# A fused fp32 model on one Trainium2 core: jobs in other places, and the S5 scan's result in PSUM

## The reference

```python
# layer 0: mixer = conv (31 taps, layernorm, silu) and retention heads, then @ w_out
# layer 1: mixer = S5, both directions, 64 groups of 16 channels, 64 complex states
for direction in (0, 1):
    bu_re = jnp.einsum('sgc,gpc->sgp', us, bb_re[direction])
    bu_im = jnp.einsum('sgc,gpc->sgp', us, bb_im[direction])
    _, _, h_re, h_im = lax.associative_scan(
        _s5_combine, (a_re, a_im, bu_re, bu_im), reverse=(direction == 1), axis=0)
    y = y + (jnp.einsum('sgp,gcp->sgc', h_re, cr[direction])
             - jnp.einsum('sgp,gcp->sgc', h_im, ci[direction]))
z = jax.nn.gelu(y + d_skip * u)
return (z @ w_glu_a) * jax.nn.sigmoid(z @ w_glu_b)
```

## Time and profile before

| | before |
|---|---|
| median of 3 executions | 1332.55 us (1329.34 to 1334.72) |
| the profiled execution, own time | 1337.0 us |
| its span | 1335.2 us, 24456 instructions |
| mean granted clock of TensorE | 0.956 |
| busy: PE, PEld | 1233.7 us (92%), 1143.0 us (86%) |
| busy: DVE, ACT, POOL | 856.9 (64%), 530.6 (40%), 410.0 (31%) |
| moved by DMA | 258.20 MB, mean 193 GB/s |

### The profile page before, as it was taken

The page is one execution under the profiler, slowest core; times in us unless marked ns, Lnnn a source line. Parts: engine busy times, 40 slices in busy tenths (PEclk is TensorE's granted clock), DMA queues, the critical chain, the costliest instruction groups (busy, mean ns, idle before and its releaser), DMA issues.

```text
span 1335.2 us, 24456 instructions
## 1 busy us (share of the span) xinstructions
PE 1233.7 (92%) x10696; PEld 1143.0 (86%) x10696; DVE 856.9 (64%) x946; ACT 530.6 (40%) x663; POOL 410.0 (31%) x573
## 2 busy tenths in 40 slices
PE   4898897999998878898999999998998999999998
PEld 4785685999998848787899999698787999999998
DVE  6699963886567558845597543556856467556553
ACT  2130232444233244343455432448267644544241
POOL 7999638398788218700000000000000012000000
PEclk7899898999998889999999999999798999999999
DMA  9962667588977645256265554345141445455551
GB/s 349 389 256 94 236 219 262 187 306 304 338 286 273 225 138 172 75 171 229 68 249 190 189 179 175 122 156 190 43 147 64 151 166 189 161 174 177 182 192 64
DMA packets 120251, 258.20 MB, mean 193 GB/s; under 512 B 5056, under 2 KB 19024, under 8 KB 120016
## 3 DMA queue, kind: packets, MB, share of 16 engines
q1 hardware_dynamic: 91184, 196.18, 41.8%
q10 hardware_dynamic: 25504, 46.81, 9.6%
q0 software_dynamic: 3456, 13.63, 2.7%
HBM read 241.93 MB, written 14.68 MB: 192 GB/s over the span
## 4 chain that ended last, share of the span: by engine, by line
PE 68%; DVE 11%; POOL 8%; DMA 5%; issue 3%; ACT 3%; SPq 1%; DVEq 0%; POOLq 0%; ACTq 0%
PE bank L1864 68%; DVE big L1403 4%; POOL tabw L714 2%; POOL tabw L711 2%; POOL big L781 2%; DMA ring<-in_w_in 1%; DMA ada_slot<-in_ada_w 1%; DVE ada_acc L1293 1%; POOL prep L719 1%; DMA ring<-in_w_fc 1%; DVE rstd L1303 1%; POOL big L774 1%; SPq L585 1%; DVE ring_split L1346 1%; ACT ada_slot_split L874 1%
## 5 line engine op out<-in xcount | busy, mean ns | idle before, releaser
L1864 PE MATMUL bank<-squares_split,ring_split 128*128 128x256 f32 x1056 | 300.7, 285 | 0.0
L1864 PEld LDWEIGHTS bank<-squares_split,ring_split 128*128 128x128 f32 x1056 | 204.5, 194 | 0.0
L787 POOL TENSOR_TENSOR y_cat<-y_cat,tmp 128x512 f32<-128x512 f32 x8 | 11.1, 1388 | 536.9 <-DVE tmp L1782 536.9
L1293 DVE SCALAR_TENSOR_TENSOR ada_acc<-ada_slot,cact,ada_acc 128x512 f32<-128x512 f32 x152 | 126.9, 835 | 5.1
L1864 PE MATMUL bank<-ada_slot_split,ring_split 128*128 128x256 f32 x432 | 122.2, 283 | 0.0
L1346 DVE TENSOR_TENSOR ring_split<-ring,ada_slot_split 128x2048 fp32r<-128x2048 f32 (+1 forms) x32 | 72.1, 2257 | 56.9 <-ACT ada_slot_split L874 56.9
L1864 PE MATMUL bank<-big_split,ring_split 128*128 128x256 f32 x352 | 100.1, 284 | 0.0
L1303 DVE RECIPROCAL rstd<-bank 128x512 f32<-128x512 f32 (+1 forms) x21 | 56.0, 2668 | 51.1 <-ACT bank L805 51.0
L1864 PE MATMUL bank<-big_split,ada_slot_split 128*128 128x256 f32 x296 | 85.5, 289 | 0.0
L1864 PEld LDWEIGHTS bank<-ada_slot_split,ring_split 128*128 128x128 f32 x432 | 82.9, 192 | 0.0
L1346 DVE TENSOR_TENSOR ring_split<-ring,tabw_split 128x2048 fp32r<-128x2048 f32 x22 | 50.4, 2291 | 49.6 <-ACT tabw_split L874 49.6
(11 more groups left out here) (420 smaller groups left out, 3879.9 us busy)
## 6 DMA issues: line engine op xcount, KB each, us to landing
...
```

Source lines behind the costliest of these rows:

```text
L1293: stt(acc, w[:, i, :], cact[:, i:i + 1], acc, ALU.mult, ALU.add)\
L1864: return pe.matmul(*args, skip_group_check=True, **kw)
```

## The change

The same work, in other places, and some in another engine or buffer.

1. *S5 loop.* The scan writes into the bank that held its own drive, DVE does both rotated products from there, POOL only the sum. v, dd and z get fixed banks, outside of the rotation; z and its reader use half a bank.
2. *S5 weights.* `wt` and `kl` are separate groups with places of their own, the first pair now ahead of `wo0.0` and the second behind `ms1`; POOL's c part waits for `kl` of the block before, and loads its input later. ACT's copies are split likewise.
3. *Projections.* `project` and `project_split` loop over input tiles outside and output tiles inside; `wo0.0/wo0.1` and `f1.0.0/f1.0.1` run as pairs. `ada7` and `ada8` follow the first pair. The inverses of `ms0`, `ms1` stay in PSUM.
4. *Start.* The first four modulation loads come in two halves, the S5 scalars before `ada_acc(4)`.
5. *Memory.* Its panel is loaded before the GLU's, its squares and mean (`mms`) come before `uu`, its norm right behind the loop. `uu` goes in two halves.
6. *GLU and norm.* `squares(3)` stand before the next split, and `KEEP_BUSY` is shorter.
7. *Second block.* `fv0`, `fv1` before `go0`; roots written to SBUF (`ROOT_PLACES`); ACT copies the linear attention's result; `nr4`, `nr5` together; two rows picked before the loop; the gates' splits use another order of buffers.

The diff, cut to its core:

```diff
-KEEP_BUSY = {"f1.0.0": 4, "uu0": 6, "ga0": 4, "ms3": 6}
+KEEP_BUSY = {"f1.0.0": 2, "uu0": 4, "ms3": 2}
...
-ADA_AFTER = {3: 10, 6: 11, 8: 12, 11: 13, 13: 14, 15: 15}
+ADA_AFTER = {3: 10, 6: 11, 8: 12, 11: 13, 15: 14}
...
-S5_AFTER = {4: 2, 10: 3, 15: 4}
-SIDE_ADA = {0: 16, 1: 17, 3: 18, 4: 19, 5: 20, 6: 21}
-SIDE_S5 = {1: 5, 3: 6, 5: 7}
+WT_AFTER = {2: 2, 6: 3, 10: 4, 14: 5}
+KL_AFTER = {4: 2, 8: 3, 12: 4}
+SIDE_ADA = {0: 15, 1: 16, 2: 17, 3: 18, 4: 19, 5: 20, 6: 21}
+SIDE_WT = {1: 6, 3: 7}
+SIDE_KL = {0: 5, 2: 6, 4: 7}
 
...
-            "wo0.0", "ada7", "wo0.1", "wt0.0", "kl0", "wt0.1", "ada8", "wo0.2", "ada9", "wo0.3", "wt1.0", "kl1", "wt1.1", "ms1"]
+            "wt0.0", "wt0.1", "kl0", "wo0.0", "wo0.1", "ada7", "ada8", "wo0.2", "ada9", "wo0.3", "ms1", "wt1.0", "wt1.1", "kl1"]
...
+            jobs.append(f"kl{SIDE_KL[b]}")
+    jobs += [f"f2.0.{p}" for p in range(4)] + ["ms2", "mms"]
...
-             "nr0", "nr1", "fk1", "cs0", "cs1", "at0", "at1", "go0", "gor0", "nr2", "nr3", "go1", "gor1",
-             "fv0", "fv1", "mq0", "mq1"]
+             "nr0", "nr1", "fk1", "cs0", "cs1", "at0", "at1", "fv0", "fv1", "go0", "nr2", "nr3", "gor0", "go1", "mq0", "gor1", "mq1"]
...
+            if name in S5_JOBS:
+                n = int(name[1:]) if name[0] != "d" else int(name[2:]) + 3
+                return bank[n % 6 if name[0] == "v" or name in ("dd0", "dd1", "dd2") else 7 if name == "dd3" else 6 + n % 2]
...
         ffn_panels(0)
+        panels.append(("mem", a["mem"].rearrange("(k p) t -> p k t", p=P), KT, T, ("memn", None)))
         for i in range(2):
             cols_panel(f"ga{i}", a["w_glu_a"], 512 * i, 512, f"ga{2 * i + 1}")
             cols_panel(f"gb{i}", a["w_glu_b"], 512 * i, 512, f"gb{2 * i + 1}")
-            if i == 0:
-                panels.append(("mem", a["mem"].rearrange("(k p) t -> p k t", p=P), KT, T, ("memn", None)))
         cols_panel("mk", a["w_mem_kv"], 0, 512, "mk1")
...
-        freed = {f"ms{n}": ("rstd", n + 1) for n in range(7)}
+        freed = {f"ms{n}": ("hn", 8 * n + 8) if n < 2 else ("rstd", n + 1) for n in range(7)}
...
+        def inverse_of(job, width):
+
+            return ps(job)[:, 0:width] if job in ("ms0", "ms1") else rs[:, 0:width]
+
+        ROOT_PLACES = {"nr0": (tabw, 0), "nr1": (tabw, 512), "nr2": (tabw, 1024), "nr3": (tabw, 1536), "gor0": (go_sq, 0), "gor1": (go_sq, 512)}
...
-                sp.dma_start(ada_slot(k), ada_source(k)).then_inc(ada_in(k)[0], 16)
+                sp.dma_start(ada_slot(k)[:, 0:4], ada_source(k)[:, 0:4]).then_inc(s(f"ada_first{k}"), 16)
+                sp.dma_start(ada_slot(k)[:, 4:8], ada_source(k)[:, 4:8]).then_inc(ada_in(k)[0], 16)
...
                 if k:
+                    job_wait(pool, f"kl{k - 1}")
                     pool.wait_ge(s("wout_out"), 16 * k)
+                if k == 0:
+                    pool.wait_ge(s("sd"), 4)
+                if k < 7:
+                    pool.dma_start(bc[(k + 1) % 2], a["s5_bc"][k + 1]).then_inc(s(f"bc_in{(k + 1) % 2}"), 16)
...
-            for n in range(17):
-                if n < 16:
-                    pool.wait_ge(s("s5p"), 2 * n + 2)
-                    if n >= 2:
-                        pool.wait_ge(s("s5g"), n - 1)
-                    pb = pbuf[n % 2]
-                    pool.tensor_tensor(wbuf[n % 2], pb[:, 0], pb[:, 1], ALU.add).then_inc(s("s5w"), 1)
-                if n >= 1:
-                    m = n - 1
-                    tab = tabs[m // 2 % 3][:, 4 * (m % 2):4 * (m % 2) + 4]
-                    pool.wait_ge(s("s5g"), m + 1)
-                    if m >= 4:
-                        pool.wait_ge(s("s5y"), m - 3)
-                    pool.tensor_tensor(rotated(m)[:, 1], gbuf[m % 2][:, :, ::-1, :], tab[:, :, 2:0:-1, :], ALU.mult).then_inc(s("s5r"), 1)
+            for n in range(16):
+                pool.wait_ge(s("s5p"), 2 * n + 2)
+                if n >= 2:
+                    pool.wait_ge(s("s5g"), n - 1)
+                pb = pbuf[n % 2]
+                pool.tensor_tensor(wbuf[n % 2], pb[:, 0], pb[:, 1], ALU.add).then_inc(s("s5w"), 1)
...
+            s5_weights_out(0)
+            s5_lags_out(0)
             for i in range(4):
                 act.wait_ge(s("lny"), i + 1)
                 act.activation(yt3[:, i, :], conv[:, i, :], ACT.Silu, bias=col("cln_b", i)).then_inc(s("yconv"), 1)
             ada_load(act, 9)
-            s5_weights_out(0)
             ada_load(act, 10)
             split_high(0)
             split_high(1)
-            squares(1)
+            squares(1, False)
+            split_high(2)
+            root("ms1")
+            shift(1)
+            s5_weights_out(1)
+            s5_lags_out(1)
             ada_load(act, 11)
-            s5_weights_out(1)
-            shift(1)
...
                     split_high(FC + u)
-                    if u in (2, 6, 10):
-                        s5_weights_out(5 + u // 4)
+                    if u in (2, 5):
+                        s5_weights_out(6 + u // 4)
                 if b >= FC2 + 3:
                     act.wait_ge(s("row_panel"), rows_before[place[f"f2.0.{b - 3}"]])
                 act.wait_ge(s("fsq_act"), 2 * b + 2)
                 act.activation(fc2_high(b), big3[:, 4 * b:4 * b + 4, :], ACT.Copy).then_inc(s("b_high"), 1)
+                if b in (2, 3, 5):
+                    s5_lags_out({2: 5, 3: 6, 5: 7}[b])
                 if b < 6:
                     ada_load(act, 16 + b)
+            act.wait_ge(s(f"panel{place['mem'] % RING}"), 16 * (place["mem"] // RING + 1))
+            for c in range(4):
+                act.activation(mem_sq[:, 512 * c:512 * c + 512].rearrange("p (k t) -> p k t", k=2),
+                               mem_x[:, 2 * c:2 * c + 2, :], ACT.Square).then_inc(s("msq"), 1)
             squares(2)
...
-            for n in range(3):
+            decay_row(0)
+            shift(2)
+            root("mms")
+            for n in (1, 2):
                 decay_row(n)
-            shift(2)
...
+            squares(3, False)
             split_high(SECOND)
+            root("ms3")
             split_high(SECOND + 1)
-            squares(3)
             shift(3)
...
             norm(0, False)
+            s5_scalars()
             ada_acc(4)
-            s5_scalars()
...
-                    if m >= 2:
-                        dve.wait_ge(s("s5r"), m - 1)
                     dve.wait_ge(s("decay"), 4 * m + 4)
-                    flat = (view.rearrange("p q c t -> p (q c t)") for view in (gbuf[m % 2], wbuf[m % 2]))
-                    result, source = flat
+                    source = wbuf[m % 2].rearrange("p q c t -> p (q c t)")
+                    result = ps(f"v{m}")[:, :]
                     dve.tensor_tensor_scan(result, decays[m % 3], source, 0.0, ALU.mult, ALU.add).then_inc(s("s5g"), 1)
                     dve.wait_ge(s("s5g"), m + 1)
                     if m >= 4:
                         dve.wait_ge(s("s5y"), m - 3)
-                    tt(rotated(m)[:, 0], gbuf[m % 2], tab[:, :, 0:1, :].broadcast_to([P, 4, 2, 64]), ALU.mult).then_inc(s("s5q"), 1)
-                if n >= 5 and n % 2:
-                    z_low((n - 5) // 2)
-            z_low(6)
-
+                    scan = result.rearrange("p (q c t) -> p q c t", q=4, c=2)
+                    tt(rotated(m)[:, 0], scan, tab[:, :, 0:1, :].broadcast_to([P, 4, 2, 64]), ALU.mult).then_inc(s("s5q"), 1)
+                    tt(rotated(m)[:, 1], scan[:, :, ::-1, :], tab[:, :, 2:0:-1, :], ALU.mult).then_inc(s("s5r"), 1)
+                if n >= 6 and n % 2 == 0:
+                    z_low((n - 6) // 2)
             split_low(GLU)
             split_low(GLU + 1)
+            z_low(6)
...
-            split_low(GLU + 2)
-
-            dve.wait_ge(s("hn"), 24)
-            rms("mms", sem="mrs")
...
+            memory_norm()
+            split_low(GLU + 2)
...
+            fox_rows(1)
             for u in range(9):
                 if u < 8:
-                    if u + 1 < 4:
-                        fox_rows(u + 1)
...
             def cat_ready(k):
                 pe.wait_ge(s("yconv") if k < 4 else s("ry"), k + 1 if k < 4 else (k - 4) // 2 + 1)
 
-            for i in range(2):
-                w = panel(f"wo{i}")
-                for j in range(2):
-                    project(f"wo0.{2 * i + j}", w, 2 * j, yt3, cat_ready, order=(4, 5, 6, 7, 0, 1, 2, 3))
-                    if (i, j) == (0, 1):
-                        s5_weights(0)
-                    if 2 * i + j < 3:
-                        ada(7 + 2 * i + j)
+            s5_weights(0)
+            s5_lags(0)
+            w = panel("wo0")
+            project_pair(("wo0.0", "wo0.1"), w, yt3, cat_ready, (4, 5, 6, 7, 0, 1, 2, 3))
+            ada(7)
+            ada(8)
+            w = panel("wo1")
+            project("wo0.2", w, 0, yt3, no_wait)
+            ada(9)
+            project("wo0.3", w, 2, yt3, no_wait)
+            mean_squares(1)
             s5_weights(1)
-            mean_squares(1)
+            s5_lags(1)
 
             for j in range(16):
```

(63 more changed lines are left out.)

261 lines of the change are left out of this document (153 added, 108 removed).

## The result

| | before | changed |
|---|---|---|
| median of 5 executions | 1332.78 us (1329.34 to 1334.72) | 1322.8 us (1321.43 to 1325.51) |
| ratio, 95% interval | | 0.9929 (0.991 to 0.9948) |
| span of the profiled execution | 1335.2 us | 1321.0 us |
| mean granted clock | 0.956 | 0.956 |
| busy: PE, DVE, POOL | 1233.7, 856.9, 410.0 us | 1214.8, 848.7, 380.8 us |

The change makes the kernel 10 us faster (0.7%), where 47 were forecast, and the time lies outside the range of 1264 to 1312 us. The two profiled executions differ by 14.2 us. `f1.0.2` starts at 247.79 us before and at 239.11 now, `f1.1.0` at 652.94 and 647.02; the window to 653.40 in the earlier trace rows ends 0.46 us behind that start.

The account below looks back on a forecast made before the run. It took PE, busy 1233.7 of 1335.2 us, as the bound. Seven stretch terms summed to -48.5 us, giving 1288.5 from the profiled execution and 1284.1 from the median; it predicted 1286, range 1264 to 1312.

Parts of the forecast that it names:

- The S5 loop: First drive to the GLU: steps of 3.65 us, 3.9 with z, take the stretch from 83.0 to 73 us, -10.
- Rival (a): S5 loop: the scan meets GpSimd's sum in each step, +17 us, 1303 us in all; chance 0.12.
- Rival (c): S5 loop: bank-sourced products slow beside GpSimd's sum, VectorE becomes the only bound, +74 us, 1360 us; chance 0.04.
- Start: Start to first output projection: -2.8 us, with 3 of GpSimd's 6.4 us wait for VectorE saved; bounds 0 and -5.
- f1.0.1: First output projection through f1.0.1: waits and half clock give -12.9, a new wait at ada8 costs 6.0; -5.2 us.
- f1.0.2 to ms2: Stretch from f1.0.2 to ms2: fewer waits and half-clock stretches, one new stall on wt7; -12.3 us, bounds -20 and -2.
- ms2 to v0: From ms2 to the first drive: h_in wait and keep-busy units save 4.7, the memory panel costs 3.5; -1.2 us.
- GLU: GLU to f1.1.0: memory panel loaded and normed early, waits on ring_split and squares go; -12 us, bounds -16 and -6.
- Second block: Second block: us2's 4.3 us wait for tabw and 3.4 of clock shrink; -5 us, bounds -9 and -1.

Follow-up runs that it names:

- z_earlier: The changed kernel with VectorE reading z(k) at the odd steps from 5 on, not the even steps from 6 on; 1294.32 us, ratio 0.9699.

## Why the prediction was wrong, point by point

**The S5 loop is the step that failed**: "with z 3.9, 16 steps 62.4". The costs in it were right. VectorE's rotated products took 0.69 us, a step of z_earlier without a reading of z took 3.75 us, and the loop measured 74.6 us without the ring where 73 was forecast. A bank as source cost nothing: 0.691 us, as with two SBUF sources and no neighbour. What it left out was a wait that the change itself adds: the even outputs of block k need z of block k-2 read, because z now lies in the accumulator's bank. The change's list names the fixed banks, and the later place of the reading stands only in the diff; the sum has no term for either and prices only the engines' work. The reading that outputs(2k) need stands on VectorE at step 2k+2. There it is behind the rotated products of step 2k+1, and PE stands still until VectorE has run two steps ahead. The next drive, v(2k+3), is behind those same outputs on PE. That one wait moved the stretch from 74.6 to 101.4 us: 26.8 of the 37 us between forecast and result. No rival named it. Rival (a), the scan beside GpSimd's sum, didn't come: one scan of 16 took 2.287 us, the first, as before. Rival (c) didn't come either. The Trainium skill, PSUM — Partial Sum Buffer, section on bank collisions, has the reason for such a wait: PE's write and VectorE's read of one bank at once are an error and are not held off by hardware, so a bank that two uses share brings a semaphore. No run here shows the error itself.

**Start, -2.8 forecast, -1.2 measured.** The direction of "GpSimd's own work gets no shorter" held, kl0's input is there at 174.8 as before. But the 3 us that I gave it of the 6.4 didn't come, since the tables ended later (146.2, where they ended at 141.5) and the x powers began at 154.84, not 153.02. The prediction also didn't ask what the early place of wt0 and kl0 costs. Without them ahead, wo0.0 starts at 161.1. The change's gains on VectorE were worth 16 us there, and the new order of two jobs took 15 of them.

**f1.0.1, -5.2 and -7.5.** The wait at ada8 came as named, 6.88 us for 6.0. It brought more half clock than the 1.7 us forecast: PE ran 10.2 us at half clock from 195.2 on and worked for 6.65 of them, which costs 3.3. Against that, the waits for normed tiles fell from 5.6 to 2.1 us, where 3.2 were left to them, and wt0 and kl0 (some 3 us of PE's work before) now stand ahead of this stretch, for which the sum had no term.

**f1.0.2 to ms2, -12.3 and -4.6.** This is the second term that failed, by 7.7 us. The stall on wt7 came as named, 3.59 us for 4. But three other waits were left or new, 4.1 us together: 2.74 for wt5, 0.73 for kl4, 0.61 for ada10. The wait for wt5:

```profile
330.80 2.92 PE L1906 MATMUL bank<-ident,tabw 64*64 64x64 f32 x64 [2.74 <-POOL tabw L738]
```

So PE's idle time fell by 3.4 us and not by 7.2. The other half is the price of the half clock. The prediction took (1 - 0.69) x 11.0 = 3.4 us for the stretch in 404 to 415, but a mean clock over a window also counts the time in which PE stands still. The half clock alone, in the kernel before:

```profile
406.40:413.20 6.80, 4.32 (x70) 4.03 (x71) 5.89 (x7) 0.86 (x2) 4.12 (x6) 0.50 0.85 343
```

PE worked for 4.32 of the 6.80 us, so the half clock cost 2.2 us there. By the same count the stretch had 6.3 us of such cost before and has 4.6 now, 1.7 less where the sum had 5.1.

**ms2 to v0, -1.2 and +3.7.** The memory's panel held ms2 for 6.0 us, where I took 3.5, with 6 as the bound. The half clock isn't the difference, 6.8 us of it lie in this stretch before and after. The memory's mean square is: its 3.6 us on PE now stand in the open, and the sum had them only as a cover for a wait.

**GLU, -12 and -14.7.** Right: both waits named are gone, 8.8 us, and the rest is clock and keep-busy work.

**Second block, -5 and -8.3.** Inside the bounds, and in part by luck. us2's wait of 4.3 us went and us0 got one of 10.0 us, which the prediction named in kind (PE arrives sooner on an unshortened chain) and had put at 2.7 (4.3 + 3.4 - 5). A wait of 4.7 us on L1303 at 929, which it didn't name, went too, and the half clock of all that follows f1.1.0 fell from 26 to 15 us.

Of the 34.3 us between forecast and profile, the loop has 28.4; the other terms, with either sign, have 5.9. Without the ring the time is 1294.32, inside the range and 8 us above the forecast: 1.6 of these are the loop's, and the other terms have most of what is left.
